# Moving the first output tile's split ahead of the last unit, loading half of w_out early in the second passes, and storing the convolution state by DMA

## The chip, the cores and the metric

The kernel runs on one NeuronCore of a Trainium2 chip. The metric is device time in microseconds (us) for one launch, the median over runs. TensorE (PE) does the matrix products, VectorE (DVE) and ScalarE (ACT) the elementwise work, GpSimd (POOL) a few of it, and SyncE (SP) issues nearly all DMAs.

## The reference, cut to what matters

```python
for l in range(2):                       # DEPTH; a prompt of 2048 tokens, a sample group of 8 x 8 tokens
    h = rmsnorm(x, g_pre)
    p = h @ w_in[l]                      # 1024 -> 3344, columns shared out to four head groups
    up = concat([conv_buf, c_c * c_x])   # A: short gated convolution, 3 taps
    a_out = c_b * conv3(up) * silu(c_z);  new_conv = up[:, -2:]
    b_out = rmsnorm(gla(q, k, v, gate)) * silu(g_z)       # B: gated linear attention
    c_out = sliding_window(q, k, v, sinks) * silu(s_z)    # C
    d_out = memory_attention(q, mem_k, mem_v) * silu(m_z) # D
    x = x + rmsnorm(concat([a_out, b_out, c_out, d_out]) @ w_out[l], g_post)
```

Among the outputs are `new_conv_p` (2 rows of 256 channels a layer) and `new_conv_s` (8 x 2 rows a layer).

## The kernel before, in words

Each layer is done in two passes over 1024 prompt tokens each, so there are four passes. The second pass of a layer also carries the 64 sample tokens (`with_sample`, or `second`). A pass has two stages: `units`, which makes the transposed mix `mix_t` (8 rows of 128 channels by the tokens), and `out`, which multiplies it with `w_out`, normalises, adds the residual and makes `h` of the next pass. Products are in float16 in three terms (high x high, high x low, low x high), so both the mix and the weights are split into a high and a low half.

The `units` stage. `UNITS` lists eight units, D0 B0 B1 C0 A0 C1 D1 A1; each is done for two token groups of 512, which gives 16 slots, numbered 0 to 15: slots 12 and 13 are D1, slots 14 and 15 are A1. The sample's part of a unit is side work of one of its slots. `plan_units` writes the order of all engines by hand from a forecast of costs: one list of items, which every engine walks, doing its own part of each. Projections (`proj`, line 1936) run ahead of the attention work and fill its waits. A slot is closed by an `end` item, in which each engine counts up its own semaphore (`step_pe`, `step_act`, `step_dve`, `step_pool`), and opened by a `begin` item, in which each engine waits for all four counts (`all_steps_done`). Unit A has next to no work of its own in its slots: its outputs are made when its projections are evicted (the convolution by DVE; the last product, of gate and convolution, in DVE's `zgate`, lines 2548 and 2551, with an ACT part of the eviction, lines 2306 and 2307). So the list of a pass ends as follows, first passes: value product of D1 in slot 13 (line 2232), zgate of A1's second token group, end 13, begin 14, end 14, `o_mix`, begin 15, end 15. In second passes the value product of D1's sample part (line 2250) stands in that place, and two `conv_out` items for A1 between begin 15 and end 15.

`o_mix` is the split of the first output tile (128 tokens): ACT writes the high half (line 2332) after all 15 earlier slots are done, DVE the low half (line 2570). `conv_out`, in second passes alone, stores the convolution state: PE transposes it (lines 1970 and 1972), ACT copies it from bank 2 (line 2338) and issues the DMA (line 2342). Unit A0's transposes stand in the middle of a pass.

Weights of `w_out` are loaded in 8 parts of 128 columns. Parts 0 to 3 lie in `first` (part of `scr`), parts 4 to 7 take the four ring places of the projection weights, `w_parts`. In first passes they are loaded raw (lines 1878 and 1896), split by ACT and DVE (lines 2328 and 2566) and kept in DRAM. In second passes the kept halves are loaded: parts 2 and 3 once 12 slots are done, each of parts 4 to 7 when the last A1 projection with the old tile in its place is done (line 1893), parts 0 and 1 once 14 slots are done (line 1876). `w_raw`, the area for raw weights, lies idle in second passes. Behind parts 2 and 3 on SP's queue stand the two loads of the sample's memory cache (line 1839), needed by `cache_t`, 16 PE transposes in slot 13 (line 2140).

The `out` stage. Its order is a list, too: `("o", t, n)` is the product of tile t with half n of `w_out` (24 matmuls, line 3012), `("xn", u)` normalises tile u of the next pass's input (ACT line 3045, DVE lines 3101 to 3113), `("h", u)` transposes it (8 PE transposes, line 3028), `("mix", t)` splits tile t. It starts with o(0,0), h(0), o(1,0), h(1), o(0,1), o(1,1). PE enters it after waiting for banks 2 to 7 to be empty. The first two x tiles and `norm_pre` are loaded once 14 slots are done (lines 1885 and 1886). The last pass makes no `h`.

Of the kernel before, what the change touches and what calls it, by code (L numbers as in the profile page):

```python
# [37 lines left out]
P = 128  # L38
# [125 lines left out]
class Forecast:  # L164
# [32 lines left out]
    def needs(self, it):  # L197
# [18 lines left out]
                 "rope_k": [("kv", n)],  # L216
                 "conv_out": [("conv", n)]}.get(k, [])
# [3 lines left out]
    def place(self, it):  # L221
# [158 lines left out]
        elif k in ("conv_out", "swa_out", "conv_in", "layer_in"):  # L380
# [7 lines left out]
    def piece_needs(self, it):  # L388

        p = self.when(("free", it["inst"] - 2), ("hi", it["tile"]))  # L390
        if it["piece"] == 2 or it["role"] == "lr":
# [7 lines left out]
         "gla_o", "gla_sq", "gla_norm", "conv_out", "swa_out")  # L399
# [4 lines left out]
def last_reader(s, row, with_sample):  # L404
# [11 lines left out]
    if u["unit"] == "A":  # L416
        if role != "x":
            return ("evict", n, "z"), u
        return ("conv_out", n, 0) if with_sample and u["st"] != 0 else ("evict", n, "x"), u
# [19 lines left out]
def plan_units(with_sample):  # L439
# [64 lines left out]
    def work(s):  # L504
# [3 lines left out]
        if kind == "A":  # L508
            if with_sample and st != 0:
                out.append(item("conv_out", [2], step=s))  # L510
        elif kind == "B":
# [65 lines left out]
    n_kept = [0]  # L577
    last_on_pe = [None]
# [135 lines left out]
    def read_noted(it):  # L714
# [10 lines left out]
        elif kind in ("score", "gla_p", "gla_fine", "gla_coarse", "gla_t", "conv_out"):  # L725
            fc.at[("read", (kind, it["step"]["n"], it.get("c", 0)))] = fc.t["PE"]
# [6 lines left out]
    def evict_next():  # L733
# [50 lines left out]
    def follow():  # L784
# [49 lines left out]
    while ended < len(slots):  # L834
        follow()
        now = fc.t["PE"]
        if running and not main and not side and not left[slots[begun]["index"]]:
# [69 lines left out]
        if "done" in it:  # L907
            waiting.append(it["done"])
            if it["done"]["unload"]:
# [28 lines left out]
def hymba_step(nc, x_prompt, x_sample, state_conv, state_gla, cache_swa_k, cache_swa_v, cache_mem_k, cache_mem_v,  # L938
# [185 lines left out]
    w_raw = sb(ctx, "w_raw", [P, RING, KT, P])  # L1124
# [72 lines left out]
    def wo_half(n):  # L1197

        whole = first if n == 0 else w_parts[:]
# [6 lines left out]
    def stores_of(it, second):  # L1206

        if it["kind"] == "conv_out":
            return int(it["step"]["g"] == 1)
# [202 lines left out]
    def units(no, l, second, build, stored_so_far):  # L1412
# [13 lines left out]
        out_c = low[64:80, 0:4 * P].rearrange("p (i g n) -> p i g n", i=2, g=2)  # L1426
# [134 lines left out]
        for it in items:  # L1561
            if it["kind"] in ("score", "turn", "value", "gla_p", "gla_t", "gla_o", "gla_sq", "rope_k", "conv_out"):
# [170 lines left out]
        def on_sync(sp):  # L1733
# [20 lines left out]
            for it in items:  # L1754
# [86 lines left out]
                elif it["kind"] == "gla_sq":  # L1841
                    s = it["step"]
                    if second and s["st"] != 0:
# [3 lines left out]
                        for h in range(2):  # L1847
# [7 lines left out]
                            sp.dma_start(dst, src).then_inc(stored, 16)  # L1855
                elif it["kind"] == "swa_out":
# [12 lines left out]
                elif it["kind"] == "o_load":  # L1869
# [5 lines left out]
                    if second:  # L1875
                        sp.dma_start(wo_of(j), kept_out(j)).then_inc(wo_in[0], 16)  # L1876
# [3 lines left out]
                elif it["kind"] == "o_x":  # L1880

                    all_steps_done(sp, n_slots - 2)
                    if build:
                        for t in range(2):
                            sp.dma_start(xl[:, t], token_rows(t, build)).then_inc(x_in[t], 16)
                        sp.dma_start(pre_g, of_layer(norm_pre.rearrange("l d -> l () d"), build[0]).to_broadcast([P, D])
                                     ).then_inc(pre_in, 16)
                elif it["kind"] == "o_wload":
# [3 lines left out]
                    if second:  # L1892
                        sp.dma_start(wo_of(j), kept_out(j)).then_inc(wo_in[1], 16)
                        continue
# [4 lines left out]
        def on_tensor(pe):  # L1899
# [4 lines left out]
            for it in items:  # L1904
# [1394 lines left out]
```

## Time and profile before

| | us |
|---|---|
| runs before | 2152.94, 2153.48, 2158.43 |
| median | 2153.48 |
| the profiled execution: its own time | 2150.82 |
| its span | 2148.7 |
| PE busy | 2047.2 (95%) |
| DVE / ACT / POOL busy | 1230.9 / 854.8 / 336.8 |
| mean granted TensorE clock | 0.981 |

The span is the time from the first to the last recorded instruction. A PE that is busy 95% of it sets the end; the other engines matter where PE waits for them.

### The profile page before, as it was taken

What the parts mean: (1) busy time and instruction counts of PE and PEld (TensorE: products, weight loads), DVE (VectorE), ACT (ScalarE), POOL (GpSimd) and SP (SyncE); (2) the same over time, 40 slices, a digit from 0 to 9 for tenths busy, and PEclk for the clock granted to TensorE, in tenths of its full rate; (3) what the DMA queues carried; (4) which work ended last, traced back from release to release, by engine and by line L of the source; (5) the groups of instructions that cost most, each with busy time, mean ns of one, the idle gap of its engine ahead of it and who ended that gap; (6) DMA issues with size and microseconds to landing.
All of it is one profiled execution on the core that took longest, in us unless ns stands there. A gap on an engine that the chain in (4) does not pass through costs nothing. (4 is left out here: it accounts for less than half of the span.)

```text
span 2148.7 us, 43406 instructions
## 1 busy us (share of the span) xinstructions
PE 2047.2 (95%) x16698; PEld 1176.4 (55%) x16698; DVE 1230.9 (57%) x2763; ACT 854.8 (40%) x1981; POOL 336.8 (16%) x267
## 2 busy tenths in 40 slices
PE   9999899989999998998999998999999999989988
PEld 4455445545566665765445444454446666656633
DVE  5467755456367754544645785555553777644433
ACT  4544333444355332343435442344434543233322
POOL 1443323001000000000133343320010000000000
PEclk9999999999999999999999998999999999999999
DMA  7431223246311122223353232213552112122332
GB/s 265 131 99 40 81 79 99 89 136 212 119 41 32 55 68 75 77 82 138 133 145 99 70 85 84 84 54 109 186 190 63 60 32 72 47 80 65 91 118 88
DMA packets 192327, 208.13 MB, mean 97 GB/s; under 512 B 53462, under 2 KB 137948, under 8 KB 192092
## 3 DMA queue, kind: packets, MB, share of 16 engines
q1 hardware_dynamic: 189012, 194.77, 29.7%
q10 hardware_dynamic: 3112, 10.59, 1.6%
q8 instruction: 135, 2.21, 0.4%
q14 instruction: 68, 0.56, 0.1%
HBM read 136.60 MB, written 57.71 MB: 90 GB/s over the span
## 5 line engine op out<-in xcount | busy, mean ns | idle before, releaser
L1936 PE MATMUL bank<-h_hi,w_parts 128*128 128x512 f16 (+4 forms) x4240 | 839.8, 344 | 16.5 <-ACTq L2311 9.8
L1936 PEld LDWEIGHTS bank<-h_hi,w_parts 128*128 128x128 f16 (+1 forms) x4240 | 403.3, 98 | 358.6 <-issue 55.8
L1936 PE MATMUL bank<-h_lo,w_parts 128*128 128x512 f16 (+3 forms) x2160 | 440.2, 343 | 2.8 <-DVEq L2562 0.5
L1936 PEld LDWEIGHTS bank<-h_lo,w_parts 128*128 128x128 f16 (+1 forms) x2160 | 205.1, 98 | 174.9 <-issue 16.5
L3012 PE MATMUL bank<-scr_h,tb_h 128*128 128x512 f16 x768 | 179.4, 393 | 14.9 <-ACT tb_h L2332 9.1
L3012 PE MATMUL bank<-w_parts,tb_h 128*128 128x512 f16 x768 | 170.3, 379 | 1.6 <-DVEq L3160 1.6
L2310 ACT ACTIVATE tb<-bank 128x512 f32<-128x512 f32 (+1 forms) x140 | 71.3, 509 | 250.0 <-PE bank L1936 229.6
L2843 POOL TENSOR_SCALAR w_raw<-w_raw 128x1024 f32<-128x1024 f32 x46 | 130.8, 2848 | 82.9 <-DMA w_raw<-in_w_in 82.5
L3012 PEld LDWEIGHTS bank<-scr_h,tb_h 128*128 128x128 f16 x768 | 76.9, 101 | 109.1 <-issue 16.0
L2443 ACT ACTIVATE scr<-bank,stat 128x256 f32<-128x256 f32 x256 | 117.4, 470 | 34.0 <-DVE stat L2789 31.4
L2463 ACT ACTIVATE scr<-bank 128x1024 f32<-128x1024 f32 x64 | 65.5, 1023 | 164.0 <-PE bank L2207 163.7
L2838 POOL TENSOR_TENSOR w_parts<-w_raw,w_parts 128x1024 f16<-128x1024 f32 x46 | 103.7, 2255 | 160.6 <-ACT w_parts L2283 160.4
L3079 ACT ACTIVATE junk<-bank 128x512 bf16<-128x512 f32 (+1 forms) x68 | 40.6, 597 | 221.7 <-PE bank L3012 209.0
L3012 PEld LDWEIGHTS bank<-w_parts,tb_h 128*128 128x128 f16 x768 | 75.0, 98 | 90.9 <-DVEq L3160 2.6
L2647 DVE COPY_PREDICATED scr<-level_mask,bank 128x128 f32<-128x128 uint8 (+1 forms) x332 | 116.8, 352 | 11.4
L2306 ACT ACTIVATE tb<-bank 128x512 f32<-128x512 f32 (+1 forms) x80 | 40.7, 508 | 147.6 <-PE bank L1936 115.2
L2859 POOL TENSOR_TENSOR stat_g<-stat_g,minus_half 128x8 f32<-128x8 f32 (+1 forms) x20 | 29.3, 1464 | 404.3 <-DVE stat_g L2695 404.3
L2803 DVE TENSOR_SCALAR scr<-scr,stat 128x256 f32<-128x256 f32 x264 | 88.0, 395 | 2.6
L2812 DVE TENSOR_TENSOR mix_t<-bank,tb 128x256 f32<-128x256 f32 x64 | 27.1, 424 | 95.4 <-PE bank L2232 94.2
L2548 DVE SCALAR_TENSOR_TENSOR tb<-tb,gate_raw 128x512 f32<-128x512 f32 (+1 forms) x80 | 49.3, 617 | 46.2 <-ACT gate_raw L2307 44.2
L2207 PE MATMUL bank<-ident,scr 128*128 128x128 f32 x512 | 69.3, 278 | 3.6 <-DVE scr L2803 3.3
L2776 DVE SCALAR_TENSOR_TENSOR bank<-bank,win_mask 128x512 f32<-128x512 f32 x64 | 44.8, 699 | 44.0 <-PE bank L2188 40.8
(300 smaller groups left out, 2700.3 us busy)
## 6 DMA issues: line engine op xcount, KB each, us to landing
w_in_kept<-w_parts SPq DMA_DIRECT2D x104, 256.0 KB, 4.3
w_parts<-w_in_kept SPq DMA_DIRECT2D x104, 256.0 KB, 2.9
w_raw<-in_w_in SPq DMA_DIRECT2D x48, 512.0 KB, 4.1
out<-scr SPq DMA_DIRECT2D x32, 512.0 KB, 2.6
scr<-in_x_prompt SPq DMA_DIRECT2D x16, 512.0 KB, 4.2
scr<-out SPq DMA_DIRECT2D x16, 512.0 KB, 4.3
rot<-out ACTq DMA_DIRECT2D x12, 512.0 KB, 3.6
mix_t<-in_x_prompt SPq DMA_DIRECT2D x8, 512.0 KB, 11.9
```

Of the source, the lines that this page charges most:

```text
L1936: m = mm(bank[b][0:m_w, 0:c1 - c0], w[:, k, 0:m_w], h[:, k, c0:c1], start=it["piece"] == 0 and k == 0, stop=it["piece"] == 2 and k == KT - 1)
L2207: m = nc.tensor.transpose(bank[b][:, (2 * h + i) * P:(2 * h + i + 1) * P], p[:, o:o + P], ident[:])
L2310: fn(part_of(s, role, pt), src, ACT.Copy, scale=scale).then_inc(tile_copied, 1)
L2443: m = fn(p[:, 256 * x:256 * x + 256], bank[6 + h][:, 256 * i:256 * i + 256], ACT.Exp, bias=z[:, 4 + x:5 + x], scale=1.0 if unit == "C" els ...
L2463: fn(pt.rearrange("p (b n) -> p b n", b=2), psum[:, 2:4, :], ACT.Copy).then_inc(bank_free[2], 1)
L2548: link(stt(z, z, 1.0, raw_gate(span, pt), ALU.add, ALU.mult))
L2647: m = nc.vector.copy_predicated(a.rearrange("p h (m i r) -> p h m i r", i=2, r=v)[:, :, :, 1, :], mask.to_broadcast([w, 2, w // (2 * v), v ...
L2776: link(stt(at[i], at[i], scale, mask.to_broadcast([P, 2, 256]), ALU.mult, ALU.add))
L2803: m = ts(p[:, n * h:n * h + n], p[:, n * h:n * h + n], z[:, at_inv + h:at_inv + h + 1], None, ALU.mult)
L2838: tt(lo_of(t), w_raw[:, t % RING, :, 0:split_width(t)], hi_of(t), ALU.subtract).then_inc(w_lo_done, 1)
L2843: nc.gpsimd.tensor_scalar(raw, raw, W_UP, None, ALU.mult).then_inc(w_scaled, 1)
L3012: m = nc.tensor.matmul(bank[b].rearrange("p (j n) -> p j n", j=RING), lhs[:, t % 2, k, :], rhs[:, :, k, :], start=j == 0 and k == 0, stop= ...
```

## The change

1. `o_mix` is put into the list as soon as 13 slots are done and A1's first token group is gated; ACT waits for these two alone.
2. In second passes all of parts 2 to 7 of `w_out` are loaded once 12 slots are done, parts 4 to 7 into `w_late`, which is `w_raw`'s memory; the out stage of second passes begins with half 1 (`fore`).
3. The x tiles are loaded once 12 slots are done, in front of what follows on SP's queue; `norm_pre` once 14 are done.
4. The out stage starts o(0), o(1) of one half, h(0), h(1), then the other half. PE waits for banks 2 and 3 in front of the first product, for banks 4 to 7 behind it, drains and then counts up `left["pe"]`. Mix 1 no longer waits for that.
5. `conv_out` becomes two 4-byte-element stores from SP for each A unit of second passes, placed right behind the eviction of x; transposes, copies and their bank use go.

```diff
@@ plan_units
-            if with_sample and st != 0:
-                out.append(item("conv_out", [2], step=s))
@@ evict_next
+        if with_sample and (ev["unit"], ev["role"]) == ("A", "x") and ev["last"]:
+            for st in groups[ev["group"]]:
+                if st["st"] != 0:
+                    emit(item("conv_out", step=st))
@@ follow
+        if not mixed[0] and ended >= len(slots) - 3 and ("evict", slots[-2]["main"]["n"], "z") in placed:
+            emit(item("o_mix"))
+            mixed[0] = True
@@ after an end item
             if with_sample and ended == len(slots) - 4:
-                for part in (2, 3):
+                for part in (2, 3, *range(RING, 2 * RING)):
                     emit(item("o_load", part=part, after=ended))
             if with_sample and ended == len(slots) - 2:
                 for part in (0, 1):
                     emit(item("o_load", part=part, after=ended))
+            if ended == len(slots) - 4:
+                emit(item("o_x", after=ended))
             if ended == len(slots) - 2:
-                emit(item("o_x"))
-            if ended == len(slots) - 1:
-                emit(item("o_mix"))
+                emit(item("o_pre", after=ended))
...
-                elif with_sample:
-                    emit(item("o_wload", part=RING + it["tile"] % RING, after=it["inst"]))
-                else:
+                elif not with_sample:
                     out_load("o_wload", RING + it["tile"] % RING, after=it["inst"])
@@ memory
-    w_raw = sb(ctx, "w_raw", [P, RING, KT, P])
+    w_raw, w_late = twice(ctx, "w_raw", F32, "w_late", F16, [P, RING, 2, KT, P], [P, RING, KT, P])
@@ units, SP
+                elif it["kind"] == "conv_out":
+                    s = it["step"]
+                    g, sample = s["g"], s["st"] == "s"
+                    sp.wait_ge(u_done, conv_steps.index(s["n"]) + 1)
+                    dst = of_layer((conv_s if sample else conv_p).rearrange("l b t d -> l (b t) d"), l)[:, P * g:P * g + P]
+                    sp.dma_start(dst.rearrange("t p -> p t"), conv_st_t[:, g] if sample else conv_tail[:, g]).then_inc(stored, 16)
...
                     if second:
-                        sp.dma_start(wo_of(j), kept_out(j)).then_inc(wo_in[0], 16)
+                        sp.dma_start(wo_of(j) if j < RING else w_late[:, j - RING], kept_out(j)).then_inc(wo_in[j // RING], 16)
@@ units, PE
                 elif kind == "end":
-                    if it["slot"] == n_slots - 1:
-                        for b in range(2, 8):
-                            pe.wait_ge(bank_free[b], plan["uses"][b])
-                        pe.drain().then_inc(left["pe"], 1)
-                    else:
-                        pe.drain().then_inc(step_pe, 1)
+                    pe.drain().then_inc(step_pe, 1)
@@ units, ACT
+                    if it["slot"] == n_slots - 1:
+                        act.wait_ge(step_pe, n_slots)
...
                 elif kind == "o_mix":
-                    all_steps_done(act, n_slots - 1)
+                    all_steps_done(act, n_slots - 3)
+                    gate_written(act, next(x["n"] for x in plan["steps"] if (x["unit"], x["g"], x["st"]) == ("A", 1, 0)))
@@ out
-        order = [("xn", 0), ("mix", 1), ("o", 0, 0), ("h", 0), ("xn", 1)] + [("split", i) for i in late]
-        order += [("o", 1, 0), ("h", 1), ("xn", 2), ("o", 0, 1), ("fin", 0), ("mix", 2), ("o", 1, 1), ("h", 2), ("xn", 3), ("fin", 1), ("mix", 3)]
+        fore, aft = (1, 0) if second else (0, 1)
+        first_o = ("o", 0, fore)
+        order = [("mix", 1), ("xn", 0), ("o", 0, fore), ("xn", 1)] + [("split", i) for i in late] + [("o", 1, fore), ("h", 0), ("h", 1)]
+        order += [("o", 0, aft), ("xn", 2), ("fin", 0), ("mix", 2), ("o", 1, aft), ("h", 2), ("xn", 3), ("fin", 1), ("mix", 3)]
@@ out, PE
+                    if x == first_o:
+                        for b in range(2, 4):
+                            pe.wait_ge(bank_free[b], plan["uses"][b])
...
                     m.then_inc(out_full[b], 1)
+                    if x == first_o:
+                        for b in range(4, 8):
+                            pe.wait_ge(bank_free[b], plan["uses"][b])
+                        pe.drain().then_inc(left["pe"], 1)
```

The `begin` items of slots 14 and 15, with their waits for all four engines, stay as they are. DVE scales `norm_pre` at `("xn", 0)` in place of at the stage's start.

## Rows read from the trace of the kernel before

**Rows 1.** The page, busy time of the engines.

```profile
PE 2047.2 (95%) x16698; PEld 1176.4 (55%) x16698; DVE 1230.9 (57%) x2763; ACT 854.8 (40%) x1981; POOL 336.8 (16%) x267
```

**Rows 2.** Groups of instructions by line: count, busy, mean ns, idle before.

```profile
L3012 PE MATMUL bank<-scr_h,tb_h 128*128 128x512 f16 x768 | 179.4, 393 | 14.9 <-ACT tb_h L2332 9.1 <-DMA scr_h<-w_out_kept 5.8
```

**Rows 3.** Timeline, end of units of pass 1: start, duration, idle before.

```profile
446.30 1.09 PE L2232 MATMUL bank<-scr,mem_v 128*64 128x128 f32 x16 [0.38 <-ACT scr L2463]
...
449.56 0.69 DVE L2551 TENSOR_TENSOR mix_t<-tb 128x512 f32<-128x512 f32 x1
...
450.83 1.06 ACT L2332 ACTIVATE tb_h<-mix_t 128x1024 f16<-128x1024 f32 x1 [2.52 <-PEq L1962]
...
451.94 7.61 PE L3012 MATMUL bank<-scr_h,tb_h 128*128 128x512 f16 x24 [4.55 <-ACT tb_h L2332]
...
460.00 1.09 PE L3028 MATMUL bank<-ident,rot 128*128 128x128 f32 x8 [0.44 <-DVE rot L3113]
```

**Rows 4.** Timeline, end of units of pass 2.

```profile
986.01 1.10 PE L2250 MATMUL bank<-scr 128*64 128x8 f32 x32
...
989.93 0.37 PE L1972 MATMUL bank<-ident,tb 128*2 128x128 f32 x1 [2.82 <-DVEq L2562]
...
995.19 7.34 PE L3012 MATMUL bank<-scr_h,tb_h 128*128 128x512 f16 x24 [3.39 <-DMA scr_h<-w_out_kept]
...
1003.24 5.34 PE L3012 MATMUL bank<-scr_h,tb_h 128*128 128x512 f16 x24
```

**Rows 5.** Timeline, end of units and first products of pass 3.

```profile
1504.95 6.77 PE L3012 MATMUL bank<-scr_h,tb_h 128*128 128x512 f16 x24 [4.55 <-ACT tb_h L2332]
...
1511.09 0.69 DVE L3101 TENSOR_SCALAR spare<-spare 128x1024 f32<-128x1024 f32 x1 [4.93 <-DMA spare<-in_norm_pre]
...
1514.19 1.54 PE L3028 MATMUL bank<-ident,rot 128*128 128x128 f32 x8 [2.47 <-DVE rot L3113]
...
1515.53 6.62 PE L3012 MATMUL bank<-scr_h,tb_h 128*128 128x512 f16 x24
```

**Rows 6.** Timeline, end of units of pass 4.

```profile
2041.44 1.10 PE L2250 MATMUL bank<-scr 128*64 128x8 f32 x32
...
2045.21 0.37 PE L1972 MATMUL bank<-ident,tb 128*2 128x128 f32 x1 [2.67 <-DVEq L2562]
...
2049.32 12.81 PE L3012 MATMUL bank<-scr_h,tb_h 128*128 128x512 f16 x48 [2.45 <-DMA scr_h<-w_out_kept]
...
2061.97 10.52 PE L3012 MATMUL bank<-w_parts,tb_h 128*128 128x512 f16 x48
```

**Rows 7.** Windows of PE: stretch, length, busy, granted clock, DMA share, GB/s.

```profile
449.50:450.00 0.50, 0.00 (x0) 0.73 0.00 0
...
2043.50:2044.00 0.50, 0.00 (x0) 0.75 0.98 401
```

**Rows 8.** Timeline, the state's transposes of A0 in pass 2.

```profile
844.62 0.27 PE L1972 MATMUL bank<-ident,tb 128*2 128x128 f32 x1
...
846.99 1.02 PE L1936 MATMUL bank<-h_hi,w_parts 128*128 128x512 f16 x4 [0.26 <-issue]
```

**Rows 9.** Windows (last two columns: DMA share, GB/s) and the transposes of the cache.

```profile
941.00:954.00 13.00, 13.00 (x100) 8.78 (x101) 7.04 (x17) 6.36 (x20) 0.00 (x0) 1.00 0.89 243
1997.00:2008.00 11.00, 11.00 (x88) 7.23 (x85) 6.00 (x14) 6.21 (x20) 0.00 (x0) 1.00 1.00 286
...
961.05 1.97 PE L2140 MATMUL bank<-ident,scr 128*128 128x128 f32 x16
...
2016.47 1.96 PE L2140 MATMUL bank<-ident,scr 128*128 128x128 f32 x16
```

**Rows 10.** Timeline: A0's convolution done; the next keys' copies; 384 4-byte elements.

```profile
818.76 0.60 DVE L2537 SCALAR_TENSOR_TENSOR spare<-spare,conv_w_t 128x64 f32<-128x64 f32 x2
...
841.35 0.51 SPq L1792 DMA_DIRECT2D rot<-tb  x1
...
1105.79 0.43 SPq L1805 DMA_DIRECT2D conv_w_t<-in_conv_w  x1
```

More of the change, by code:

```diff
@@ L379, in place @@
             run("PE", 0.9 if unit == "C" else 1.1, self.needs(it))
-        elif k in ("conv_out", "swa_out", "conv_in", "layer_in"):
+        elif k == "conv_out":
+            self.issue(2, when(("conv", n)))
+        elif k in ("swa_out", "conv_in", "layer_in"):
             p = run("PE", 0.4, self.needs(it))
@@ L398 @@
 ON_PE = ("proj", "gate", "rope_k", "cache_t", "score", "turn", "value", "value_part", "gla_p", "gla_t", "gla_kv", "gla_s",
-         "gla_o", "gla_sq", "gla_norm", "conv_out", "swa_out")
+         "gla_o", "gla_sq", "gla_norm", "swa_out")
 STATS = 4
@@ L418, in last_reader @@
             return ("evict", n, "z"), u
-        return ("conv_out", n, 0) if with_sample and u["st"] != 0 else ("evict", n, "x"), u
+        return ("evict", n, "x"), u
     reader = {"B": dict(q=("gla_p", n, end), k=("gla_p", n, end), v=("gla_t", n, end - 1), z=("gla_norm", n, 0)),
@@ L508, in work @@
         if kind == "A":
-            if with_sample and st != 0:
-                out.append(item("conv_out", [2], step=s))
-        elif kind == "B":
+            return out
+        if kind == "B":
             chunks = 1 if sample else ST // CH
@@ L577, in plan_units @@
     n_kept = [0]
+    mixed = [False]
     last_on_pe = [None]
@@ L1195, in wo_lo_of, with wo_half @@
         return wo_of(j)[:, 1]
-    def wo_half(n):
-        whole = first if n == 0 else w_parts[:]
+    def wo_half(n, second):
+        whole = first if n == 0 else w_late[:] if second else w_parts[:]
         return whole[:, :, 0], whole[:, :, 1]
@@ L1208, in stores_of @@
         if it["kind"] == "conv_out":
-            return int(it["step"]["g"] == 1)
+            return 1
         if it["kind"] == "gla_sq":
@@ L1561, in units @@
         for it in items:
-            if it["kind"] in ("score", "turn", "value", "gla_p", "gla_t", "gla_o", "gla_sq", "rope_k", "conv_out"):
+            if it["kind"] in ("score", "turn", "value", "gla_p", "gla_t", "gla_o", "gla_sq", "rope_k"):
                 att_uses[(it["kind"], it["step"]["n"], it.get("c", 0))] = it["banks"]
@@ L1880, in on_sync @@
                 elif it["kind"] == "o_x":
-                    all_steps_done(sp, n_slots - 2)
+                    all_steps_done(sp, it["after"])
                     if build:
@@ L1885, in on_sync @@
                             sp.dma_start(xl[:, t], token_rows(t, build)).then_inc(x_in[t], 16)
+                elif it["kind"] == "o_pre":
+                    all_steps_done(sp, it["after"])
+                    if build:
                         sp.dma_start(pre_g, of_layer(norm_pre.rearrange("l d -> l () d"), build[0]).to_broadcast([P, D])
@@ L2329, in on_scalar @@
                 elif kind == "o_mix":
-                    all_steps_done(act, n_slots - 1)
+                    all_steps_done(act, n_slots - 3)
+                    gate_written(act, next(x["n"] for x in plan["steps"] if (x["unit"], x["g"], x["st"]) == ("A", 1, 0)))
                     fn(m_hi[:, 0], mix_t[:, :, 0:P], ACT.Copy, scale=M_UP).then_inc(mh_done, 1)
-                elif kind == "conv_out":
-                    s = it["step"]
-                    i = 1 if s["st"] == "s" else 0
-                    rows = 2 * NB if i else 2
-                    filled(act, it, 2)
-                    link(fn(out_c[0:rows, i, s["g"], :], bank[2][0:rows, 0:P], ACT.Copy))
-                    act.drain().then_inc(bank_free[2], 1)
-                    if s["g"] == 1:
-                        dst = conv_s if i else conv_p
-                        act.dma_start(of_layer(dst.rearrange("l b t d -> l (b t) d"), l),
-                                      out_c[0:rows, i].rearrange("p g n -> p (g n)")).then_inc(stored, 16)
                 elif kind == "gate":
@@ L2988, in on_tensor @@
         def on_tensor(pe):
-            for x in order:
+            for i, x in enumerate(order):
                 if x[0] == "o":
@@ L3051, in on_scalar @@
                     if t == 1:
-                        for e in ("pe", "dve"):
-                            act.wait_ge(left[e], no)
+                        act.wait_ge(left["dve"], no)
                     if t >= 2:
-                        act.wait_ge(out_full[out_bank(t, 1)], t // 2)
+                        for n in range(2):
+                            act.wait_ge(out_full[out_bank(t, n)], t // 2)
                     fn(m_hi[:, t % 2, :, 0:out_size(t)], mix_t[:, :, tcols(tile_at[t])], ACT.Copy, scale=M_UP).then_inc(mh_done, 1)
@@ L3098, in on_vector @@
             n_root = n_low = 0
-            if build is not None:
-                dve.wait_ge(pre_in, 16)
-                link(ts(pre_g, pre_g, H_UP, None, ALU.mult))
             for x in order:
@@ L3120, in on_vector @@
                     if t >= 2:
-                        dve.wait_ge(out_full[out_bank(t, 1)], t // 2)
+                        for n in range(2):
+                            dve.wait_ge(out_full[out_bank(t, n)], t // 2)
                     m_low = m_lo[:, t % 2] if r == P else m_hi[:, t % 2, :, r:2 * r]
```

25 lines of the change are left out of this document (7 added, 18 removed).

## Prediction

> **What bounds the kernel now.** I read the page's busy times first: PE is busy 95% of the span and no other engine over 57% [rows 1]. So only time in which PE waits, or runs slowly, can be won. Next the groups by line: all 768 products with the half in `scr_h` waited 14.9 us together, nearly all of it at the first product of a pass, for the first tile's split and for the last parts of `w_out` [rows 2]. Then the timeline at the four places where `units` ends and `out` begins, which is where the change acts. In each, the reader sees PE's last work of the units, a hole, and 24 products that take longer than the usual 5.34 us [rows 3 to 6]. Last the windows, for the clock and the DMA rate [rows 7, 9].
>
> The holes, from the end of PE's last unit work to the first product: pass 1 from 447.39 to 451.94, 4.55 us [rows 3]; pass 2 from 987.11 to 995.19, 8.08 us [rows 4]; pass 3 up to 1504.95, 4.55 us [rows 5]; pass 4 from 2042.54 to 2049.32, 6.78 us [rows 6]. They end differently: in passes 1 and 3 with ACT's split, in 2 and 4 with the landing of parts 0 and 1 of `w_out`.
>
> **Part 1, the split ahead.** The code tells what PE waits for once the split is out of the way. The `begin` items of slots 14 and 15 still make PE wait until every engine has closed slots 13 and 14, and DVE closes slot 13 behind the last zgate, which stands before end 13 in the list. In pass 1 that zgate ends at 450.25 and ACT, which waits for the same 15 slots, starts its split at 450.83 [rows 3]. In passes 2 and 4 the little transpose of `conv_out` stands right behind begin 15 on PE, so its start, 989.93 and 2045.21, is the moment at which PE gets through [rows 4, 6]. So the title's step does not let PE run on: the first product starts there, not at the end of PE's last unit work. For passes 1 and 3 I set it 0.25 us behind the start of the old split, or 0.86 us before the old first product [rows 3, 5]. That is 2 x 0.86 = 1.7 us. The moved split itself costs ACT 1.06 us and DVE about 1.2 us right behind slot 12, with DVE and ACT between attention steps; nothing for PE, and up to 1 us a pass if these were not idle.
>
> **Part 2, w_out early.** In pass 2 the first product moves from 995.19 to 989.93, 5.26 us; in pass 4 from 2049.32 to 2045.21, 4.11 us [rows 4, 6]. Parts 0 and 1 are issued as before and land by about 995.2 and 2049.2, and half 0 is now needed two products later, over 10 us behind the new start: hidden, with 5 us to spare.
>
> What it costs: at the start of slot 12 SP now issues 4 more parts of 512 KB, in pass 2 also two x tiles of 512 KB, in front of the memory cache of the sample. PE's transposes of that cache have a fixed place. The queue took 13 us for 3.15 MB in pass 2 (243 GB/s) and 11 us in pass 4 (286 GB/s); the transposes came at 961.05 and 2016.47, 7.1 us and 8.5 us behind the end of these stretches [rows 9]. Pass 4: 2.1 MB more is 7.3 us at 286 GB/s: hidden, barely. Pass 2: 3.15 MB more is 11.0 us at 286 GB/s and 13.0 us at 243, so the cache is late by 3.9 or 5.9 us if the added transfers run no faster than the mix of before. They have 4 KB rows, the cache 512-byte ones, so I take a faster rate and 2 us; bounds 0 and 5.9 us. What is queued behind the waiting transposes is all of PE.
>
> On this a rule of the Trainium skill (DMA: Bandwidth & Descriptors, Specifications) gives a limit of about 358 GB/s of HBM traffic for a core. By that figure 3.15 MB takes an estimated 8.8 us, and the stall would be 1.7 us; the sum would change by 0.3 us. No stretch of rows 9 reaches that rate.
>
> **Part 3 and 4, the order of out.** In pass 1 h(0) waited 0.44 us for its input [rows 3]. In pass 3 it waited 2.47 us, since `norm_pre` was first used at 1511.09; its 8 transposes took 1.54 us in place of about 1.04, and the 24 products behind them 6.62 us in place of 5.34, at a lowered clock [rows 5, 4]. With o(1) in front of h(0), 5.2 us more lie before it, so the wait goes: 0.44 + 2.47 + 0.50 + 1.28 = 4.7 us. Mix 1 has to be ready for o(1): it follows the end of DVE's unit work by about 1.1 + 1.2 us, and the first product covers 5.2 us. The loads of `post_g` and of the residual wait for `left["pe"]`, now behind the first product, some 3 us later than before; their first use is behind the third product, so they stay hidden. The drain behind the first product is new: PE waits for its last matmul and fills again. A matmul takes 393 ns and one follows another each 0.22 us [rows 2, 4], so 0.2 to 0.5 us, I take 0.3; four times, 1.2 us lost.
>
> **Part 5, the state by DMA.** At A1 the transposes stood in the hole: counted already. At A0 they cost 0.27 us each and some 0.25 us of waiting around each [rows 8], 1.04 us a pass, 2.1 us in all; between 0 and 2.1. The stores replace them. SP spent 0.43 us on a load of 384 4-byte elements [rows 10]; 2048 elements are 5.3 times that, 2.3 us, and with the prompt's 256 some 2.6 us for one A unit. They can go when A0's convolution is done, at 819.4 in pass 2, 22 us ahead of the copies of the next unit's keys at 841.35 [rows 10]: hidden. The row bounds issue alone; how long the stores hold the DMA engines no row shows. Without cover each us too much would be a us of PE, since the rotation waits for those copies.
>
> The Trainium skill (the same page and section) says that transfers under 512 B are done as read-modify-write. It gives no time for one, and no row here shows such a write, so the sum stays.
>
> **The clock.** The first products of the four passes took 2.27, 2.00, 1.43 and 2.29 us over the full rate (24 products take 5.34 us, 48 take 10.52) [rows 3 to 6], 8.0 us. The granted clock fell to half, 1.2 GHz, some 2.3 us after PE had stopped in pass 1 and 1.2 us in pass 4 [rows 7], and again after the 2.47 us wait of pass 3 [rows 5]. The new holes are 3.7, 2.8, 3.7 and 2.7 us, each longer than that wait, so I let the same 8.0 us stand. Bounds: 8.0 won if the clock holds in all four, 3 lost if it comes back later.
>
> **Sum.** Won: 1.7 + 5.3 + 4.1 + 4.7 + 2.1 = 17.9 us. Lost: 1.2 (drains) + 2.0 (cache) = 3.2 us. Net 14.7 us off 2150.8 us, the profiled execution's own time, which gives 2136.1. It lies 2.7 us below the median of the runs, 2153.5, so for the median I say 2138.8 us.
>
> **Rivals.**
> A, PE runs on: if `begin` didn't hold PE, the holes would go nearly whole, 4.55 + 8.08 + 4.55 + 6.78 = 24.0 us in place of 11.1, and the clock's 8.0 us with them: some 21 us more than forecast, 2118 us. The holes' lengths speak for it, the list of items against it. Chance 0.05.
> B, as forecast, but the shorter holes keep the clock up in most passes: 5 to 8 us more, about 2132 us. The fall only 1.2 us into the hole of pass 4 speaks against it [rows 7]. Chance 0.17.
> C, the cache is late in both second passes: at 243 GB/s 5.9 us in pass 2 and 0.1 in pass 4; if the 4 KB rows brought no more than 200 GB/s, 8.6 and 2.0 us. With drains of 0.5 us and no gain at A0 (3 us more) the net gain is 3 to 8 us: about 2148 us, most of it no change that can be told. The saturated queue speaks for it [rows 9]. Chance 0.13.
> D, on the other side: the 4-byte stores hold SP and the queue. A pair has 2304 elements and 22 us of cover; at 15 ns an element one behind another it takes 35 us, and the keys of C1 come 13 us late in each second pass: 25 us lost against 14.7 won, 2164 us. It decides from 22 + 7.4 us for a pair, 13 ns an element. For it speaks that no row shows such a store; against it that 384 elements were issued in 0.43 us, 1.1 ns each [rows 10]. Chance 0.05.
> The forecast itself has 0.60, with a range of its own from 2134 to 2144.
>
> **How the numbers follow.** 2138.8 us is the likeliest case. From 2128 to 2149 holds the forecast, B and most of C; it leaves out A, D and the edge of C. Under 0.3%, 6.5 us, this kernel's runs tell nothing from no change. Faster by more: forecast, B and A, less a part for what I have not seen, 0.81. Within: 0.13, from C. Slower: 0.06, from D.
>
> **What would show it.** The first product of passes 1 and 3 follows DVE's last zgate by under 1 us, with its split long done; that of passes 2 and 4 names no DMA. PE is still idle before it, 3.7, 2.8, 3.7 and 2.7 us. h(0) waits for nothing. PE's transposes of the cache (line 2140 of before) wait for a DMA in the second pass of layer 0 if I am right on its price, and not in that of layer 1. The prediction is wrong if they wait over 6 us, if the clock stays at full rate across the holes, or if the key copies of C1 wait for SP.

## The result, and the profile after

| | us |
|---|---|
| before, median of 4 runs beside the changed kernel | 2153.2 (2151.3 to 2158.4) |
| changed kernel, median of 4 runs | 2175.1 (2171.5 to 2177.3) |
| ratio, 95% interval | 1.0106, 1.0089 to 1.0122 |
| changed kernel: profiled execution, span, clock | 2171.5, 2168.9, 0.979 |

The change made the kernel slower by 1.1%, some 22 us, where 14.7 us less was forecast. The page of the changed kernel, against [rows 1]:

```profile
PE 2055.8 (95%) x16690; PEld 1180.4 (54%) x16690; DVE 1230.1 (57%) x2763; ACT 851.8 (39%) x1973; POOL 335.8 (15%) x267
```

PE has the 8 transposes less that went, but is busy 8.6 us longer; a part of it is work at a lowered clock, as the window from 838 to 840 below shows. I set each PE row of the two timelines beside its like; the difference of their starts grows by 7.3 us in each second pass behind unit A0, by 3.1 and 4.5 us behind A1 and by 2.0 us at the memory cache, and shrinks where `out` begins. It also grows by about 3 us between 150 and 300 us, in pass 1, to which I come back in experiment 8. Line numbers from here on are those of the kernel named.

**Behind the stores.** Changed kernel, second pass of layer 0: SP's queue, then the timelines of PE, ACT and DVE.

```profile
823.19 0.39 SPq L1867 DMA_DIRECT2D out<-conv_tail  x1
824.43 0.39 SPq L1867 DMA_DIRECT2D out<-conv_st_t  x1
827.77 2.87 SPq L1768 DMA_DIRECT2D w_parts<-w_in_kept  x2
...
832.12 1.53 PE L2162 MATMUL bank<-scr 64*32 64x128 f32 x24
838.06 0.85 PE L2162 MATMUL bank<-scr 64*32 64x128 f32 x8 [4.40 <-issue]
...
838.25 0.38 ACT L2302 ACTIVATE tb<-bank 128x256 f32<-128x256 f32 x1 [6.30 <-remote]
...
838.93 0.43 DVE L2537 SCALAR_TENSOR_TENSOR tb<-tb,gate_raw 128x256 f32<-128x256 f32 x1 [5.41 <-ACT gate_raw L2303]
```

PE stops inside one run of 32 matmuls of line 2162, after the 24th. "issue" says that it waited for nothing that the profile shows. SP paid 0.39 us for each store (0.34 for each wide one of experiment 3). The next two loads took it 2.87 us to issue, where a pair takes 0.81. The windows of that stretch, first of the changed kernel, then of experiment 3, in which the same bytes are stored in wide pieces (columns: window, us, busy and count of PE, PEld, DVE, ACT, POOL, clock, DMA share, GB/s):

```profile
824.00:826.00 2.00, 1.71 (x12) 0.99 (x11) 1.75 (x9) 0.00 (x0) 0.00 (x0) 1.00 0.30 3
826.00:828.00 2.00, 1.90 (x16) 1.70 (x17) 1.75 (x4) 0.71 (x1) 0.00 (x0) 1.00 1.03 2
828.00:832.00 4.00, 4.00 (x42) 3.03 (x40) 2.76 (x9) 2.34 (x10) 0.00 (x0) 1.00 0.26 1
832.00:834.00 2.00, 1.46 (x25) 0.96 (x25) 1.46 (x6) 0.00 (x0) 0.00 (x0) 1.00 0.22 19
834.00:838.00 4.00, 0.00 (x0) 0.00 (x0) 0.00 (x0) 0.00 (x0) 0.00 (x0) 0.62 1.00 48
838.00:840.00 2.00, 1.94 (x16) 1.40 (x16) 0.43 (x1) 0.66 (x2) 0.00 (x0) 0.50 0.67 33
```

```profile
826.00:828.00 2.00, 2.00 (x26) 1.55 (x25) 1.66 (x7) 0.82 (x4) 0.00 (x0) 1.00 0.91 260
...
834.00:838.00 4.00, 4.00 (x36) 2.49 (x35) 1.49 (x5) 1.67 (x8) 0.47 (x2) 1.00 0.07 16
```

From 834 to 838 no engine does anything, the DMA engines are occupied the whole time, and they move 48 GB/s; in experiment 3 the same pair of loads ran at 260. The clock then fell to half and stayed there for PE's next 2 us and more. The three other places, in PE's timeline (A1 of layer 0, A0 and A1 of layer 1; their sample stores were issued at 984.32, 1888.63 and 2045.08):

```profile
996.82 0.71 PE L2203 MATMUL bank<-ident,scr 128*128 128x128 f32 x2 [2.59 <-issue]
...
1899.24 0.27 PE L2162 MATMUL bank<-scr 64*32 64x128 f32 x1 [1.89 <-issue]
1902.00 0.37 PE L2162 MATMUL bank<-scr 64*32 64x128 f32 x1 [2.49 <-issue]
...
2056.52 0.37 PE L2162 MATMUL bank<-scr 64*32 64x256 f32 x1 [2.03 <-issue]
```

**The cache and the start of `out`.** PE's timeline of the changed kernel, against [rows 9] and [rows 3 to 6]:

```profile
975.64 1.97 PE L2136 MATMUL bank<-ident,scr 128*128 128x128 f32 x16 [1.92 <-DMA scr<-in_cache_mem_v]
...
450.94 1.09 PE L2228 MATMUL bank<-scr,mem_v 128*64 128x128 f32 x16 [0.38 <-ACT scr L2452]
455.93 12.49 PE L3007 MATMUL bank<-scr_h,tb_h 128*128 128x512 f16 x48 [3.90 <-PEq L1969]
482.77 2.55 PE L3007 MATMUL bank<-scr_h,tb_h 128*128 128x512 f16 x11 [1.37 <-DVEq L3161]
...
1003.77 1.10 PE L2246 MATMUL bank<-scr 128*64 128x8 f32 x32
1008.29 12.84 PE L3007 MATMUL bank<-w_late,tb_h 128*128 128x512 f16 x48 [3.41 <-PEq L1969]
1035.47 1.90 PE L3007 MATMUL bank<-scr_h,tb_h 128*128 128x512 f16 x8 [1.37 <-DVEq L3161]
...
1514.51 1.09 PE L2228 MATMUL bank<-scr,mem_v 128*64 128x128 f32 x16 [0.38 <-ACT scr L2452]
1519.53 13.21 PE L3007 MATMUL bank<-scr_h,tb_h 128*128 128x512 f16 x48 [3.92 <-PEq L1969]
1547.09 3.19 PE L3007 MATMUL bank<-scr_h,tb_h 128*128 128x512 f16 x14 [1.36 <-DVEq L3161]
```

The first product follows PE's last unit work by 3.90, 3.41, 3.92 and, in pass 4, 2.89 us; none names a DMA. In pass 1 it starts 1.04 us behind the end of DVE's last zgate (454.89). New is the wait of 1.37 us at 482.77, 1035.47 and 1547.09: it is o(2,0), waiting for DVE's fin(0).

### The profile page after: what moved, and what is told of

It reads as the page before. It is cut to its first block and busy times, and to the rows that moved or that the text cites. A ratio compares the mean times of both kernels' runs of the same rounds, so it can differ in the third digit from the quotient of the medians.

```text
span 2168.9 us, 43423 instructions
## 1 busy us (share of the span) xinstructions
PE 2055.8 (95%) x16690; PEld 1180.4 (54%) x16690; DVE 1230.1 (57%) x2763; ACT 851.8 (39%) x1973; POOL 335.8 (15%) x267
## 5 line engine op out<-in xcount | busy, mean ns | idle before, releaser
L3007 PE MATMUL bank<-scr_h,tb_h 128*128 128x512 f16 x768 | 174.0, 386 | 12.1 <-PEq L1969 7.8
L3007 PE MATMUL bank<-w_late,tb_h 128*128 128x512 f16 x384 | 89.2, 391 | 8.2 <-PEq L1969 6.3
L3007 PE MATMUL bank<-w_parts,tb_h 128*128 128x512 f16 x384 | 85.2, 379 | 0.0
L2203 PEld LDWEIGHTS bank<-ident,scr 128*128 128x128 f32 x512 | 58.1, 145 | 22.6 <-issue 13.2
```

The lines of the kernel that those rows point to most:

```text
L2203: m = nc.tensor.transpose(bank[b][:, (2 * h + i) * P:(2 * h + i + 1) * P], p[:, o:o + P], ident[:])
L3007: m = nc.tensor.matmul(bank[b].rearrange("p (j n) -> p j n", j=RING), lhs[:, t % 2, k, :], rhs[:, :, k, :], start=j == 0 and k == 0, stop= ...
```

## The experiments

Times are set beside runs of the kernel before on the same chip (medians 2150.8 to 2151.6).

**1. The transposes back.** The changed kernel with `conv_out` of before, on all engines.

```diff
-                elif it["kind"] == "conv_out":            # SP: two stores of 4-byte elements
+                elif kind == "conv_out":                  # PE, ACT, as in the kernel before
+                        m = nc.tensor.transpose(bank[2][0:2 * NB, 0:P], conv_st_t[:, s["g"], :], ident[:])
```

> The changed kernel, with the convolution state stored as before (PE transposes, ACT copies, one DMA a layer); all else of the change stays. Theory S (the 4-byte-element stores cost the time: PE stands still without a semaphore behind each pair of them, 7.3 us behind unit A0 in each second pass, 3.1 and 4.1 us behind A1): the changed kernel's median of 2175.1 less 21.8 us, plus 2.1 us for the transposes at A0, about 2155 us, and if the 4.2 us that it lost within the first 280 us of pass 1 are of that one execution, 2151 us; the four stalls named issue at the sample's scores (line 2162) are gone. Theory B (the new start of the out stage or the early loads cost the time): 2172 to 2177 us, stalls still there. Theory C (another place of the code in memory, the instruction supply is late wherever the listing has changed): stalls at other places, 2165 to 2175 us.

2151.9 us, ratio 0.9996 (0.9986 to 1.0006). No wait named issue stands at the sample's scores any more. The stores were 1.1% of the kernel; theories B and C fall.

**2. Only the stores**, in the kernel before.

> The kernel before, with only the convolution state's path changed: two 4-byte-element stores by SP for each A unit of second passes. Theory S: 2153.2 + 21.8 - 2.1 = 2173 us, with the stalls named issue at the sample's scores 8 to 13 us behind each pair of stores. Theory B: 2151 to 2154 us. Theory C: stalls, but not tied to the stores.

2186.8 us, ratio 1.0167 (1.0148 to 1.0185), so 36 us and not 20. The waits of PE in that kernel (total, times, longest):

```profile
PE bank L3000 <- DMA scr_h<-w_out_kept: 14.9, 2, 7.8
...
PE bank L2249 <- ACT scr L2449: 7.3, 1, 7.3
```

In the order of before the last parts of `w_out` stand right behind A1's stores, and PE is soon to need them: it waited 14.9 us for them in place of 5.8 (3.39 and 2.45) [rows 4, 6]. The early loads of the change hid a part of its own damage.

**3. Wide pieces.**

```diff
-                    sp.dma_start(dst.rearrange("t p -> p t"), conv_st_t[:, g] if sample else conv_tail[:, g])
+                    sp.dma_start(dst.rearrange("(p t) -> p t", p=P), conv_st_t[:, g] if sample else conv_tail[:, g])
```

> The changed kernel, with the same bytes stored at the same place by the same queue, but each partition's 2 or 16 values side by side in DRAM: pieces of 8 and 64 bytes, 256 for a pair of stores in place of 2304 pieces of 4 bytes (the state outputs then have another layout than the reference's). Theory S, cost by the piece: a ninth of 21.8 us is left, 2.4 us; about 2155 us. Theory S', cost by the byte or by there being a write among the loads: 2170 to 2175 us. If the stores cost nothing (theories B, C): 2175 us.

2148.4 us, ratio 0.9988 (0.9976 to 1.0000). Neither the bytes nor a write at that place cost anything that can be told; the shape of the stores does. The edit changes three things at once: the number of pieces, their size, and that neighbours in DRAM come from different partitions. Experiment 7 takes them apart in part. From the transposes' place at A0 no time was won against experiment 1: PE's offset to the kernel before grew there by 0.2 us in pass 2 and 0.1 in pass 4 with the transposes, and by 0.2 and 0.0 without.

**4. PE runs on.** Experiment 1 with three edits.

```diff
                 elif kind == "begin":
-                    all_steps_done(pe, it["slot"])
+                    if it["slot"] < n_slots - 2:
+                        all_steps_done(pe, it["slot"])
@@ out
-        order += [("o", 0, aft), ("xn", 2), ("fin", 0), ("mix", 2), ("o", 1, aft), ("h", 2), ("xn", 3), ("fin", 1), ("mix", 3)]
+        order += [("xn", 2), ("o", 0, aft), ("fin", 0), ("mix", 2), ("o", 1, aft), ("h", 2), ("xn", 3), ("fin", 1), ("mix", 3)]
```

The third edit: parts 4 to 7 and the x tiles stand behind `begin` 12 in the list, whose SP part loads the memory cache, and not ahead of it.

> The first experiment's kernel with three more edits: PE no longer waits for all engines at the begin items of slots 14 and 15; xn(2) stands before the third product again; in second passes the memory cache is loaded before parts 4 to 7 of w_out and the x tiles. Against the first experiment: 3 x 1.37 us for o(2,0) = 4.1, 2.0 for the cache, and the first product of each pass starts right behind PE's last work of the units, 2.9 to 3.9 us earlier, less some 0.5 us at o(1) which waits for mix 1, about 12 us in all; 0 to 8 us more if the clock then holds. So 2127 to 2137 us if the first experiment gives 2155. Rival: banks 2 and 3 come free only when the last value product and the zgates are done, so the product starts under 1 us earlier: 2145 to 2149 us.

2132.8 us, ratio 0.9911 (0.9897 to 0.9924). PE's timeline at the end of pass 1's units:

```profile
448.45 1.09 PE L2233 MATMUL bank<-scr,mem_v 128*64 128x128 f32 x16 [0.38 <-ACT scr L2468]
450.16 10.80 PE L3023 MATMUL bank<-scr_h,tb_h 128*128 128x512 f16 x48 [0.62 <-ACT w_parts L2332]
```

The hole is 0.62 us, and 48 products with a drain take 10.80 us: the clock held. In second passes PE still stood 2.66 and 2.2 us at the second transpose of A1's state, for ACT.

**5. The stores from ACT's queue.**

```diff
-                    sp.dma_start(dst.rearrange("t p -> p t"), conv_st_t[:, g] if sample else conv_tail[:, g])
+                    act.dma_start(dst.rearrange("t p -> p t"), conv_st_t[:, g] if sample else conv_tail[:, g])
```

> The changed kernel, with the same 4-byte-element stores issued by ACT, so that they stand in another queue than SP's loads. Theory E (the pieces occupy the DMA engines that all queues, the instruction supply among them, share): the same stalls, 2170 to 2180 us, and the loads of SP behind them as slow as before (about 40 GB/s). Theory Q (the damage is done by what stands behind the stores in SP's own queue): the loads go through at 250 GB/s and the stalls go, 2150 to 2157 us.

2177.6 us, ratio 1.0121 (1.0106 to 1.0136). SP's loads now took 0.80 us to issue, but still ran at 47 GB/s from 834 to 838, which is theory E's sign. "Issuing engines are not separate DMA queues" (the Trainium skill, DMA: Bandwidth & Descriptors) says that DMAs of all issuing engines end on the same 16 DMA engines; by that rule, the trace agrees.

The equal time is in part a coincidence. ACT waits for the convolution in front of its stores, and PE waits for ACT, once in each second pass:

```profile
822.22 0.21 ACT L2421 ACTIVATE stat<-stat 128x4 f32<-128x4 f32 x1 [10.39 <-DVEq L2528]
...
824.53 2.08 PE L2177 MATMUL bank<-rot,tb 64*128 64x128 f32 x16 [4.38 <-ACTq L2436]
```

So at A0 PE's offset grows by some 6.3 us through the edit's own wait and by 1.1 and 2.2 us behind the stores, in place of 7.3 each. PE's waits named issue at the sample's scores come to 1.0 us in place of 11.0; behind A1 they stand, 1.9 and 2.7 us. That the stalls are the same, as theory E said, is shown for A1 alone.

**6. The stores in the out stage.** A0's are issued behind y(1), A1's behind y(4), on a semaphore of their own.

> The changed kernel, with the 4-byte-element stores of second passes moved into the out stage: those of unit A0 behind the store of output tile 1, those of A1 behind that of tile 4. There PE runs products of 128x512 one after another, 216 ns each, and needs few instructions in a microsecond. Theory I (the stalls are late instructions): few or no stalls named issue, 2150 to 2160 us. Theory L (any transfer beside the stores is late, loads of tiles too): the x tiles and residual tiles of the out stage come late, and PE waits for them in place of instructions, 2165 to 2180 us. The stalls at the sample's scores go in either case.

2155.4 us, ratio 1.0014 (1.0004 to 1.0025): 6 to 7 us over experiment 3, 20 under the changed kernel. SP's queue, DVE and PE of its second pass:

```profile
1068.38 0.33 SPq L2935 DMA_DIRECT2D out<-scr  x1
1068.76 0.43 SPq L2940 DMA_DIRECT2D out<-conv_tail  x1
1069.23 0.84 SPq L2940 DMA_DIRECT2D out<-conv_st_t  x1
1074.58 0.57 SPq L2943 DMA_DIRECT2D scr<-in_x_sample  x1
...
1086.68 1.28 DVE L3158 SCALAR_TENSOR_TENSOR scr<-bank,st_o,scr 64x1024 f32<-64x1024 f32 x1 [1.69 <-DMA scr<-in_x_sample]
...
1088.15 8.10 PE L3006 MATMUL bank<-w_late,tb_h 128*128 128x512 f16 x24 [3.31 <-DVEq L3160]
```

No wait named issue is left in these stretches. What is left goes through data: the sample's residual lands 12 us behind its issue, fin waits for it, PE for fin, and the clock falls for the product behind. Behind A0's sample store, issued at 1033.93, the load that waits for the store of y(1) went only at 1045.41. Both theories are right in part.

**7. Only the prompt's pieces.** The sample's state is stored as in experiment 3.

> The changed kernel with only the prompt's state (256 pieces for a unit) stored in 4-byte pieces, the sample's 2048 values a unit in 128 pieces of 64 bytes (and so in another layout than the reference's). Cost by the piece, in proportion: 384 of 2304 pieces are left, 17% of the about 27 us between the changed kernel and the variant with wide pieces, that is 4 to 5 us: 2153 us. If there is a threshold (instructions held ahead cover a short hold of the DMA engines): no cost, 2148 us. If each store costs a fixed time whatever its size: half, 2161 us.

2150.2 us, ratio 0.9997 (0.9988 to 1.0007), 1.9 us over experiment 3 with intervals that overlap; no stall named issue at the scores. A fixed time per 4-byte store is excluded, and so is a cost of the 4-byte size by itself: 256 such pieces a unit are left. Proportion and threshold are not told apart. Nor is the number of the sample's pieces from their order in DRAM: no run here stored its 2048 pieces of 4 bytes in another order.

**8. ACT free of the wait in front of A1's copies.**

> The fourth experiment's kernel, where ACT in second passes no longer waits for all engines at the begin item of slot 14, so that it empties the bank between the two transposes of the convolution state of A1. Those transposes waited 2.7 and 2.2 us for ACT, and the first product another 0.5 us. Without it 2 x 3 us go, and up to 2 x 2.3 us of lowered clock: 2122 to 2127 us. Rival: the first copy or the second transposition then waits for DVE's convolution of the sample, and nothing is won: 2131 to 2134 us.

2133.0 us, ratio 0.9914. A miss of the experiment, not of the theory: the edit was in a second branch for `begin`, which the first branch of that name hides, so this was the program of experiment 4 again. It is of use as a repeat: PE's rows of the two stand 2.1 us apart at the end of pass 1, with medians 0.2 us apart. Between 150 and 300 us the one lost 1.5 us on the kernel before and the other 0.6; all thirteen traces, the changed kernel's with 3.2 among them, lost from 0.2 to 3.8 us there, whatever their edits. I take it for what one execution differs from another by, the one of before being a quick one; the two of one program differ by 1 us of it.

**9. ACT free, in the right branch.**

```diff
                 elif kind == "begin":
-                    all_steps_done(act, it["slot"])
+                    if it["slot"] < n_slots - 2:
+                        all_steps_done(act, it["slot"])
```

> The fourth experiment's kernel, where ACT too no longer waits for all engines at the begin items of slots 14 and 15 (the edit of the experiment before this one touched a branch that is never reached, so that it repeated the fourth kernel). The second transpose of A1's convolution state waited 2.7 and 2.2 us for ACT's copy of the first, and the first product another 0.5 and 0.4 us. With ACT free it waits some 0.6 us: 2 x 2.4 = 5 us less, and up to 2 x 2.5 us if the clock then holds over the product: 2123 to 2128 us against 2132.9. Rival: the out stage's first product then waits for something else that is ready only with DVE's last zgate, and mix 1 comes no earlier, so that o(1) waits for what o(0) won: 2130 to 2133 us.

2127.2 us, ratio 0.9890 (0.9876 to 0.9904). The hole of second passes, in which the two transposes stand, is 2.0 us (983.30 to 985.32) and 1.8 in pass 4, but 48 products still take 12.42.

**10. Experiment 1 with xn(2) in its old place.**

> The first experiment's kernel with one edit: xn(2) stands before the third product in the out stage's list, as before the change, in place of behind it. If DVE's xn(2) work, now behind ACT's share of the third product, is what made o(2,0) wait 1.37 us in three passes: 4.1 us less than the first experiment, about 2148 us, ratio 0.998, and these three waits gone. Rival: tile 2 of x is late in either order (its load waits for h(0)), and the wait stays: 2152 us.

2147.0 us, ratio 0.9980 (0.9969 to 0.9991), 3.4 us under experiment 1. Of four waits for fin, 5.8 us together, only the one that the kernel before has too remains, 1.7 us. The place of xn(2) was the cause.

**11. A0's stores 85 us later.** The changed kernel; SP waits for 11 slots in front of them.

> The changed kernel, with A0's 4-byte-element stores held back until 11 slots are done, some 90 to 110 us later, to a stretch of units where SP's queue has less to do; A1's stay. Theory R (the pieces hurt only where an engine's next block of instructions, or a load that is awaited, happens to fall due within the 10 to 15 us behind them): A0's share, some 15 us in two passes, shrinks to 0 to 8 us: 2160 to 2168 us, and the stall at the sample's scores of C0 is gone. Theory F (every pair of stores stops the engines for its own 4 to 7 us, wherever it stands in the units): the stall moves with the stores, 2173 to 2177 us.

2165.0 us, ratio 1.0064 (1.0044 to 1.0084): 9 us less. PE's offset grew by 5.9 us in pass 2 and 2.8 us in pass 4 in the new place, in place of 7.3 each. The stall at the sample's scores of C0 is gone, and the new one is ACT's and DVE's (SP's queue, then ACT):

```profile
909.63 0.39 SPq L1873 DMA_DIRECT2D out<-conv_st_t  x1
915.17 3.75 SPq L1772 DMA_DIRECT2D w_parts<-w_in_kept  x2
...
924.42 1.02 ACT L2458 ACTIVATE scr<-bank 128x1024 f32<-128x1024 f32 x1 [6.61 <-remote]
```

So the stall moves with the stores, and its price depends on what falls due there: between the two theories, nearer R.

**12. Turned by DVE, in pieces of 128 bytes.** Experiment 9, where the sample's 16 and the prompt's 2 columns lie side by side in `conv_all` (128 x 32 for a unit).

```diff
+                elif kind == "conv_out":                  # DVE, once a unit
+                        link(nc.vector.transpose(conv_turn[:, g], conv_all[:, g]))
+                        dve.drain().then_inc(conv_turned, 1)
@@ SP
+                    for k in range(P // 32):
+                        for dram, at, n in ((conv_s, 0, 2 * NB), (conv_p, 2 * NB, 2)):
+                            dst = of_layer(dram.rearrange("l b t d -> l (b t) d"), l)[:, P * g + 32 * k:P * g + 32 * k + 32]
+                            sp.dma_start(dst, conv_turn[32 * k + at:32 * k + at + n, g]).then_inc(stored, 16)
```

> The ninth experiment's kernel (PE and ACT run on through the last two slots, xn(2) in its old place, the memory cache first), with the convolution state neither turned by PE nor stored in 4-byte pieces: DVE transposes 32x32 blocks of it, once a unit in second passes, and SP stores it in pieces of 128 bytes, 72 for a unit, by 8 DMAs. The hole before the first product of second passes was 2.0 us, and the product's 48 matmuls took 1.9 us more than at the full rate. If nothing else holds PE, the hole shrinks to some 0.5 us: 3 us less, and up to 3.8 us more if the clock then holds: 2120 to 2124 us against 2127.2. Rival: the first product waits for the last eviction out of banks 2 and 3 in place of the transposes, or 8 issues of 0.4 us on SP make a load late: 2126 to 2130 us.

2123.2 us, ratio 0.9869 (0.9853 to 0.9886): 28 us less than before and 51 less than the changed kernel. One line's instructions (ns min/median/max), then PE at the end of pass 2's units:

```profile
L2545 DVE STREAM_TRANSPOSE conv_turn<-conv_all x4: 211/212/213, 814.0 to 2007.1; 128x32 f32<-128x32 f32 x4
```

```profile
981.53 1.10 PE L2257 MATMUL bank<-scr 128*64 128x8 f32 x32
983.23 10.80 PE L3025 MATMUL bank<-w_late,tb_h 128*128 128x512 f16 x48 [0.60 <-issue]
```

The clock now holds in every pass: 10.80 us for 48 products behind holes of 0.60 to 0.62 us. DVE's turn costs 0.21 us a unit and nobody waits for it.

## Why the prediction was wrong

**The step that failed is Part 5, "hidden".** I priced the stores by SP's issue, 2.6 us for a unit, and looked for who waits for SP; "how long the stores hold the DMA engines no row shows" stood there as a gap without a bound. Issue was even cheaper, 0.39 us a store. What the runs show is a hold: from the issue of the sample's store to the first work behind the stall, 13.6, 12.5, 13.4 and 11.4 us at the four places (824.43 to 838.06, 984.32 to 996.82, 1888.63 to 1902.00, 2045.08 to 2056.52), 14.8 us in experiment 11, and 11.5 in experiment 6 up to the issue of the load that waited (1033.93 to 1045.41). Shared out over 2304 pieces that is 5 to 6.4 ns a piece, where issue had suggested 1.1. Against the place where I set a price, the key copies 22 us behind, this is still hidden; rival D, which decides at 13 ns, did not come about either. It named the right operation and a figure not far off, 2164 us, but the waiter was another: the loads that stand in those 12 to 15 us, and PE, ACT and DVE themselves. The loss was 23.7 us by ratios (1.0106 less 0.9996), where nothing was forecast and 0.05 given. I should have bounded the hold from above, and asked what stands in each 15 us behind the stores.

**That it is the engines' instructions which come late is inferred, and the traces speak for and against it.** For it: the stop inside a run of equal matmuls with no semaphore, all engines standing, no such stop in `out`, where PE takes 4.6 matmuls a us, and this answer for the DMA queues of the changed kernel from 1896 to 1899 (packets, MB, share of 16 engines), in the stall of pass 4:

```profile
q8 instruction: 1, 0.02, 15.6%
```

One packet of the instruction queue took 7.5 us (0.156 x 3 x 16); over the whole kernel before, 135 take 0.4% of 2148.7 x 16, about 1 us each. None there takes over 2.0 us and none in experiment 3 over 1.8, while experiment 2, which has the same stores, has one of 5.7 us (from 837.26) and one of 6.9 us (from 1911.68). "Instruction fetch mechanics" (the Trainium skill, Runtime: NRT & Kernel Launch) says that each engine's instructions are fetched in blocks of 16 KB by a DMA queue of its own, mostly hidden; the packet's size agrees. Against it: at all four places PE runs again before the next such packet has landed. The one of 7.5 us starts at 1898.84 and ends at 1906.3, and PE runs from 1902.00; at the other three, PE runs from 838.06, 996.82 and 2056.52, and the next packet starts at 842.92, 1000.71 and 2061.91. So the packets of this queue are late, but none is seen to end a stall. Also against it, or open: behind A1's stores in pass 2 the trace has no DMA activity at all from 990 to 998, while PE stops within it. What is occupied then, the memory's side of 2304 small writes or something else, no run here tells.

**A0's transposes (2.1 us won): wrong, nothing.** Their 1.04 us were taken up by the waits next to them (experiments 1 and 3).

**The first products: right.** Holes of 3.7, 2.8, 3.7 and 2.7 us were forecast, 3.90, 3.41, 3.92 and 2.89 measured. `begin` did hold PE, as the list of items said; rival A needed experiment 4's edit. h(0) waits for nothing.

**The sum at the four starts: right in size, but for one wait.** From the end of the last unit work to o(2,0), before and after: 30.82 and 30.74 us, 33.42 and 30.60, 33.69 and 31.49, 29.79 and 25.6 (its fifth product starts 48 matmuls of 0.216 us behind 2082.22). That is 9.3 us won; without the three new waits of 1.37 us it is 13.4, against 14.6 forecast (1.7 + 5.3 + 4.1 + 4.7 - 1.2). The wait was missed because I followed PE's order and not DVE's and ACT's: in the new list xn(2) stands behind the third product, so DVE reaches fin(0) only after 2.3 us of xn(2).

**The clock: right, with some luck in the size.** The first 48 products took 2.0, 2.3, 2.7 and 2.0 us over 10.52, 8.9 us with four drains, 8.0 and 1.2 forecast. The same holes stand in five more traces (experiments 3, 5, 6, 7 and 11), and there it was 11.1, 11.6, 9.7, 11.2 and 10.1 us. Rival B did not come: the clock held behind holes of 0.6 us, not behind those of 1.8 and 2.0 (experiments 12 and 9).

**The cache: right.** 2.0 us forecast in pass 2 and nothing in pass 4; 1.9 and nothing measured, 1.6 and 1.5 in experiments 1 and 3. Rival C is out. With the cache ahead in the queue (experiments 4, 9 and 12) the wait is gone.

Without the stores' stalls the sum would have been 9.3 us at the starts less 1.9 for the cache, 7.4 us. Experiment 3, which is just that, gained 2.6 us by its ratio, at most 5.2 by its interval. In its trace the four starts gave 7.2 us and not 9.3, since the lowered clock took 2.1 us more (11.1 against 8.9); less 1.5 for the cache, 5.7 us. The rest was lost in stretches of passes 1 and 3 (1.7 us between 140 and 300, 2.6 us between 1100 and 1490) that the change does not touch, and in which executions of one program differ by 1 to 2 us. Whether some of these 3 us are the change's all the same stays open.

## What to carry to other kernels

A DMA's price lies in its pieces too, and it is paid by loads and engines up to 15 us behind it: before an operation is called hidden, bound how long it holds the shared path, not how long it takes to issue. In this kernel, an engine that stopped in the middle of a run of equal instructions, with "issue" as its releaser and the others standing as well, was a sign to look 10 to 15 us back on all DMA queues. And where a stage's first work is ready early, look at whether a wait written for other reasons still stands in front of it: taking those waits off PE and ACT was worth more than any part of the change, because the clock then held as well.

## What was not expected of the hardware

- 2304 pieces of 4 bytes, 9 KB, hold up loads and engines for 11.4 to 14.8 us, and PE stops only 8.7 to 9.9 us behind the issue. Below 512 bytes transfers are read-modify-write (the Trainium skill, DMA: Bandwidth & Descriptors, Specifications), but pieces of 8, 64 and 128 bytes, also below it, cost nothing that could be told, with 256 of them for a unit in experiment 3 and 72 in experiment 12. The size against 512 did not decide here; the count may have, or the order in DRAM (experiment 7).
- Loads beside them fell from 260 to 48 GB/s, and to 47 where ACT had issued the stores.
- The same edit cost 36 us in one order of loads and 24 in another (experiments 2 and 1).
- A 128x32 block turn on DVE takes 0.21 us, against two PE transposes, two ACT copies and their waits.
